# Three orders changed in a TensorE-bound chain of blocks: group norm at the scan's end, sums of a norm, fillers in windowed attention

## The reference, cut to what matters

```python
for i in range(DEPTH):                       # first block, DEPTH = 2
    if i < N_A_LAYERS:
        h = h + mamba2_mixer(h, ...)         # 4 groups: conv, chunked scan, gated group norm, out projection
    else:
        k_sh, v_sh = shared_kv(h, ...)
        h = h + swa_layer(h, k_sh, v_sh, ...)    # windowed attention, window 128, 16 heads
    h = h + per_layer_embedding(h, p[i], ...)    # sigmoid(rms_norm(h) @ gate_w) * (p_i @ proj_w)
# group norm of the mixer, per group of 512 channels
yg = yg * lax.rsqrt(jnp.mean(yg * yg, axis=-1, keepdims=True) + EPS)
# second block begins
h = rms_norm_2(x, ln1_g[i]); z = h @ w_in[i]
```

## Time and profile before

| | |
|---|---|
| median of 3 runs | 1419.25 us (1418.35 to 1421.17) |
| profiled execution | 1417.13 us |
| its span, first to last instruction | 1415.0 us |
| TensorE, matmuls busy | 1376.1 us, 97% |
| VectorE, ScalarE, GpSimd busy | 836.4, 661.4, 527.2 us |
| mean granted TensorE clock | 0.995 |

### The profile page before, as it was taken

The page is one execution under the profiler, slowest core; times in us unless marked ns, Lnnn a source line. Parts: engine busy times, 40 slices in busy tenths (PEclk is TensorE's granted clock), DMA queues, the critical chain, the costliest instruction groups (busy, mean ns, idle before and its releaser), DMA issues.

```text
span 1415.0 us, 18159 instructions
## 1 busy us (share of the span) xinstructions
PE 1376.1 (97%) x6776; PEld 1088.3 (77%) x6776; DVE 836.4 (59%) x1453; ACT 661.4 (47%) x1126; POOL 527.2 (37%) x259
## 2 busy tenths in 40 slices
PE   9999999999999999989999999999999999999998
PEld 6777878777778878856888887775677888888887
DVE  5576464757557764675576514367756654544755
ACT  6654634635455443585555412344555323232553
POOL 2553553635320034455100434124353555555200
PEclk9999999999999999999999999999999999999999
DMA  5322323222123223211334333130012323333331
GB/s 187 90 75 60 90 60 88 77 60 75 62 88 90 91 89 90 75 49 43 89 90 119 90 119 119 31 104 30 16 30 81 99 91 103 91 103 91 118 89 60
DMA packets 33078, 116.82 MB, mean 83 GB/s; under 512 B 3932, under 2 KB 4316, under 8 KB 32736
## 3 DMA queue, kind: packets, MB, share of 16 engines
q1 hardware_dynamic: 31976, 111.85, 26.2%
q10 hardware_dynamic: 1016, 3.81, 0.8%
HBM read 113.55 MB, written 2.10 MB: 82 GB/s over the span
## 4 chain that ended last, share of the span: by engine, by line
PE 88%; DVE 5%; ACT 3%; issue 2%; POOL 1%; DMA 1%; ACTq 0%; DVEq 0%
PE bank L1272 84%; PE bank L1730 1%; PE bank L1573 1%; ACT wsh L846 1%; DMA h<-in_xT 1%; POOL wsl L698 1%; DVE arena L1888 0%; PE bank L1445 0%; POOL arena L756 0%; PE bank L1480 0%; ACT arena L1208 0%; DVE arena L2260 0%; ACT arena L928 0%; DVE arena L1968 0%; POOL arena L779 0%
## 5 line engine op out<-in xcount | busy, mean ns | idle before, releaser
L698 POOL TENSOR_TENSOR wsl<-ring,wsh 128x1024 fp32r<-128x1024 f32 x144 | 349.6, 2429 | 569.0 <-ACT wsh L846 568.9
L846 ACT ACTIVATE wsh<-ring 128x1024 fp32r<-128x1024 f32 x199 | 210.6, 1058 | 493.3 <-PE bank L1272 470.8
L1272 PE MATMUL bank<-parts1h,wsh 128*128 128x512 f32 (+1 forms) x736 | 293.2, 398 | 8.2 <-DVE parts1l L1811 2.1
L1272 PE MATMUL bank<-parts0h,wsh 128*128 128x512 f32 x704 | 282.9, 402 | 3.7 <-issue 1.3
L1272 PE MATMUL bank<-parts1l,wsh 128*128 128x512 f32 (+1 forms) x736 | 286.3, 389 | 0.0
L1272 PE MATMUL bank<-parts1h,wsl 128*128 128x512 f32 (+1 forms) x736 | 286.2, 389 | 0.0
L1272 PE MATMUL bank<-parts0h,wsl 128*128 128x512 f32 x704 | 275.0, 391 | 0.0
L1272 PE MATMUL bank<-parts0l,wsh 128*128 128x512 f32 x704 | 274.7, 390 | 0.0
L1272 PEld LDWEIGHTS bank<-parts1h,wsh 128*128 128x128 f32 x736 | 138.9, 189 | 44.3 <-issue 4.3
L1272 PEld LDWEIGHTS bank<-parts0h,wsh 128*128 128x128 f32 x704 | 132.6, 188 | 38.4 <-issue 6.8
L1272 PEld LDWEIGHTS bank<-parts1h,wsl 128*128 128x128 f32 x736 | 138.9, 189 | 29.0
(11 more groups left out here) (313 smaller groups left out, 1823.1 us busy)
## 6 DMA issues: line engine op xcount, KB each, us to landing
ring<-in_wstream SPq DMA_DIRECT2D x206, 512.0 KB, 3.6
arena<-in_alibi ACTq DMA_DIRECT2D x2, 1024.0 KB, 5.1
outT<-arena SPq DMA_DIRECT2D x8, 256.0 KB, 2.6
h<-in_xT SPq DMA_DIRECT2D x2, 256.0 KB, 5.8
h<-in_xT ACTq DMA_DIRECT2D x2, 256.0 KB, 6.3
h<-in_xT SPq DMA_DIRECT2D x1, 512.0 KB, 8.5
h<-in_xT ACTq DMA_DIRECT2D x1, 512.0 KB, 9.3
arena<-in_cmpb ACTq DMA_DIRECT2D x1, 496.0 KB
```

The lines of the kernel that those rows point to most:

```text
L698: return nc.gpsimd.tensor_tensor(dst, src, hi.bitcast(F32), ALU.subtract)
L846: nc.scalar.activation(wsh[n % NSET][:, :], src, ACT.Copy).then_inc(*done("high", ("high", L)))
L1272: return nc.tensor.matmul(*args, **kw)
```

## The change

Three orders and one split of a step:

- Scan of group 3: `sout(2, 4)` moves into the scan's fillers. With nine fillers in place of eight they are spread anew, which puts `sout(2, 1)` ahead of `ssd2(3, 0)`, and `proj(3, 9)` and `psp(0)` each earlier by a step (`psp(0)` now ahead of `ssd2(3, 3)`). After the scan: `yt` x4, `sout(2, 5)`, `ya`, `sout(2, 6)`, `gn`, `sout(2, 7)`, `pp(0, 0)`, `gb`, `pp(0, 1)`, `pp(0, 2)`, `pp(0, 3)`. Before, it was `yt` x4, `sout(2, 4)` to `sout(2, 7)`, `gn`, `pp(0, 0)`, `pp(0, 1)`, `gb`, `pp(0, 2)`, `pp(0, 3)`.
- All groups: the last `yadd` leaves `gn` for a new step `ya`, one step after the beginning of `head`.
- Attention: `psp(1)` moves from behind the `aV` of unit 1 to ahead of the first `aT`; the four fillers `pp(1, m)` move from units 3, 4, 5, 6 to units 1, 2, 8, 9.
- `norm(4)` moves from behind `avg(0)` to behind `avg(1)`, `nb(4)` from behind `avg(1)` to behind `avg(2)`.

```diff
-            fill = nxt[7:8] + so[:2] + nxt[8:9] + so[2:4] + nxt[9:] + [("psp", 0)]
-            head, mid, tail = so[4:], [("pp", 0, 0), ("pp", 0, 1)], [("pp", 0, 2), ("pp", 0, 3)]
+            fill = nxt[7:8] + so[:2] + nxt[8:9] + so[2:4] + nxt[9:] + [("psp", 0)] + so[4:5]
+            head, mid, tail = so[5:7], so[7:] + [("pp", 0, 0)], [("pp", 0, m) for m in (1, 2, 3)]
...
-        out += [("yt", g, m) for m in range(GT)] + head + [("gn", g)] + mid + [("gb", g)] + tail
+        out += [("yt", g, m) for m in range(GT)] + head[:1] + [("ya", g)] + head[1:] + [("gn", g)] + mid + [("gb", g)] + tail
...
-    out += [("gate", 6)] + swa[:7] + [("gate", 7), ("qT", 1)]
-    between = {3 + m: [("pp", 1, m)] for m in range(4)} | {10 + m: [("ao", 0, m)] for m in range(6)}
+    out += [("gate", 6)] + swa[:7] + [("gate", 7), ("qT", 1), ("psp", 1)]
+    between = {u: [("pp", 1, m)] for m, u in enumerate((1, 2, 8, 9))} | {10 + m: [("ao", 0, m)] for m in range(6)}
...
-    out += body[:k] + [("psp", 1), ("half",)] + body[k:]
+    out += body[:k] + [("half",)] + body[k:]
...
-    out += [("avg", 0), ("norm", 4), ("avg", 1), ("nb", 4), ("avg", 2), ("avg", 3)] + [("cmp_in", 0), ("mif",), ("mrow",), ("cmp_in", 1)]
+    out += [("avg", 0), ("avg", 1), ("norm", 4), ("avg", 2), ("nb", 4), ("avg", 3)] + [("cmp_in", 0), ("mif",), ("mrow",), ("cmp_in", 1)]
...
-                if k == "gn":
+                if k == "ya":
                     yadd(a[0], 3)
```

## The result

The change makes the kernel faster: a median of 1411.41 us over 8 executions (1410.03 to 1415.96) against 1419.19 us over 8 of the kernel before (1416.42 to 1422.34), a ratio of 0.9943 with a 95% interval of 0.9931 to 0.9955. By the medians that is 7.8 us; 6.1 were predicted, 1413.1 us with a range of 1410.5 to 1417.0.

What follows compares the result with a forecast made beforehand. TensorE, busy 97% of the span, was taken as the bound, leaving its idle time and clock falls to gain. Scan 2.6, attention 1.3 and norm 4 2.2 sum to 6.1 us, giving a 1413.1 us median; range 1410.5 to 1417.0.

Steps and rivals of the forecast that it cites:

- `ssd2(3,0)`, 1.3 us: Scan of group 3: sout(2,1) ahead covers the 1.32 us wait for the masked decay; gain 1.3 us.
- `ssd3(3,3)`, a wait of 0.9 again: Scan of group 3: psp(0)'s subtraction now precedes the scaled term, so TensorE again waits 0.9 us; gain 0.
- `gn`, a wait of 1.5 against 1.47: End of group 3's scan: the last sum comes sooner but so does TensorE; wait 1.5 us against 1.47, gain 0.
- The clock falls at `gn` as before: After gn(3): the quiet stays as long (1.5 + 1.1 us), so the clock falls as before; gain 0, other end 1.7 us.
- `gb` to `sout(3,0)`, 1.3 us: Broadcast to sout(3,0): a third pp of 1.37 us fills the 1.3 us idle; gain 1.3 us.
- Attention, 1.3 us: Attention: 0.9 in the first units plus 1.5 at units 8 and 9, less 1.1 new idle in units 3 to 6.
- Norm 4, 2.2 us: Norm 4: 0.58 us idle before the sums goes and the clock holds, worth 1.6; gain 2.2 us, bounds 0.4 and 2.3.
- Rival 1: Clock holds at gn(3) as well: 1.7 us more gain, 1411.4 us; chance 0.17.
- Rival 2: Clock falls at norm 4 anyway, behind the two column sums: 1.7 us less gain, 1414.8 us; chance 0.15.
- Rival 3: Attention's unfilled units cost more than 1.1 us, latencies setting their pace: 3.5 us idle, 1415.6 us; chance 0.14.
- Rival 4: Attention's four unfilled units take 18.9 us without fillers too, losing 5.5 us: 2.4 us slower, 1421.7 us; chance 0.05.
- Rival 5: Moved steps only move the waits; just ssd2(3,0)'s 1.3 and the 0.6 between norm 4's sums stay: 1417.4 us; chance 0.07.

Runs made afterwards that it cites:

- Experiment 4: Kernel after with psp(0) moved one step later, behind ssd2(3,3): 1410.32 us, ratio 0.9934 against the kernel before.
- experiment 7: Kernel after without ya, the last sum of squares made at gn again: 1413.28 us, ratio 0.9951 against the kernel before.
- experiment 10: Kernel after with psp(1) one step later, behind the aT of unit 0: 1412.14 us, ratio 0.9946 against the kernel before.
- experiment 1: Kernel before with only the scan's new order and the step ya: 1414.53 us, ratio 0.9964 against the kernel before.
- Experiment 6: Kernel after with attention's four fillers back at units 3 to 6, psp(1) still early: 1414.04 us, ratio 0.9957 against the kernel before.
- experiment 8: Kernel after with attention's second filler at unit 5 in place of unit 2: 1410.84 us, ratio 0.9936 against the kernel before.
- experiment 2: Kernel before with only attention's new order: 1416.15 us, ratio 0.9981 against the kernel before.
- Experiment 5: Kernel after with gn(3) behind sout(2,7) again, ya staying where it is: 1411.72 us, ratio 0.9941 against the kernel before.
- experiment 9: Kernel after with psp(0) behind ssd2(3,3) and attention's fillers at units 1, 5, 8, 9: 1408.33 us, ratio 0.9924 against the kernel before.
- experiment 11: Kernel after with psp(0) behind ssd2(3,3), fillers at units 1, 5, 8, 9 and psp(1) behind unit 0's aT: 1408.43 us, ratio 0.9922 against the kernel before.
- experiment 3: Kernel before with only norm 4's new order: 1415.95 us, ratio 0.998 against the kernel before.

## Why the prediction was right, and where it was off

The direction and the places held, and the total came out. Of the three terms the scan's held in size (2.6 against 2.7), attention's was too small by 0.8 us, and norm 4's was too large by 0.65 in an execution without the fall. Those two errors cancel, so that the total is closer than its parts deserve, by luck. Step by step:

- **`ssd2(3,0)`, 1.3 us.** Right: no idle before it.
- **`ssd3(3,3)`, a wait of 0.9 again.** Right: 0.75, and for the reason given, the subtraction in front of the term. Experiment 4 shows it: with the subtraction behind the term the wait is 0. The chain to the last sum shortens with it, and the wait before `gn` falls from 1.25 to 0.70.
- **`gn`, a wait of 1.5 against 1.47.** Right in kind, 1.24 measured. That the two canceled was no accident: TensorE comes a block earlier and so does the sum, and experiment 7 shows the part that `ya` has in that (0.6 us).
- **The clock falls at `gn` as before.** True of this pair of profiles, but no property of the kernels. The old order fell in two of three profiled executions, the order of after in two of five (after and experiment 10; not in experiments 1, 6 and 8), and in the pair of after and experiment 1 it cost 1.6 us; in experiment 2, where it lasted twice as long, it cost 3.2. With the chance of 0.17 given to the other case the prediction was surer than one profile allows.
- **`gb` to `sout(3,0)`, 1.3 us.** Right: no stall behind the third `pp`. Experiment 5 shows that what stands between `gn` and `gb` matters as well: with `pp(0,0)` alone there, and a split ahead of the root, the broadcast waits 1.86 us.
- **Attention, 1.3 us: the term that was mis-sized.** It measured 2.09.
  - The opening gave waits of 1.61 + 0.23 = 1.84 where 1.7 + 0.7 = 2.4 were worked out: the step "It waits 0.7" before `aT(1,0)` was too much by 0.5. From the start of the first `aV` to that `aT` the product was to take 5.0 us and took 4.7 (601.88 to 606.60), and TensorE's own work was to take 4.3 and took 4.5: a `pp` between `aS` and `aV` takes 1.58 us from its first matmul to that of the `aV` (604.12 to 605.71 and 608.68 to 610.26 in after), and the prediction had 1.37, from a block of such matmuls.
  - Units 8 and 9 gave back all of their 2.0 us and not 1.5. The units without fillers lost 1.79 us and not 1.1; VectorE's busy time of 14.47 us was only a bound from below for their pace: the waits in after end with ScalarE's copy (L1100) and GpSimd's product (L756), the last links of a chain over all the engines.
  - By the listed waits the net is 5.48 - 3.86 = 1.6 us. Most of the other 0.5 lies in the distances between TensorE's starts: at a listed wait the distance grows by some 0.07 us (once 0.14) more than the idle that is listed, of which before has one wait more, and before has three delays of 0.1 to 0.2 us that are too short for the list (at 605.84, 609.92 and 632.62) where after has one. Counted by starts, before loses 6.4 us there and after 4.4.
  - Experiment 6 shows which half made the gain: the fillers (1.6 to 2.0), hardly the earlier `psp(1)` (0.45 at most).
- **Norm 4, 2.2 us.** 2.16 in the profiled pair. But the prediction's 0.58 of idle and 1.6 of clock hold only for an execution with the fall. Without it the old order has 0.58 before the sums and 0.70 before the broadcast, and the part is worth 1.55. The diagonal's margin in the new order was worked out as 0.8 us; the diagonal is there at 757.79 (757.10 and 0.69) and TensorE comes at 758.67, 0.9 later. Two splits and the two small transfers stood ahead of the root on ScalarE, and it held all the same.
- **The sum.** 6.1 predicted; 6.9 by the three segments of the profiled pair, 6.4 with no falls, 6.7 at equal clocks.

The prediction weighed a rule of the Trainium skill (TensorE: Matmul & The Clock Gate, Part 1: The HAM clock gate), that the activity window runs freely and does not restart with the kernel. The runs agree with it: the order of before fell at norm 4 in one profiled execution and, in experiments 1 and 2, which have the same order there, did not. They show that the same order falls in some executions and not in others; that a free-running window is the reason they do not show. By that rule the sum was to be 4.4 us, with the whole fall taken off. Without falls it came to 6.4: attention gave 0.8 more than its term, and at norm 4 the old order pays 0.70 us at the broadcast when the clock holds, so that a fall there costs it 0.6 us and not 1.7.

Rival 1 came about in three of five profiles of the new order. Rival 2 did not in any of ten. Rival 3 was right in kind: the unfilled units cost more than 1.1 us, and what their waits end with is not VectorE; its size, 3.5 us, was too much. Rivals 4 and 5 did not come about. Rival 4 needed 4.8 us lost in the four units, and those show 1.8 us of idle in all. (The window of 18.10 us was chosen to span them with work around them; it isn't the same work as the 18.9 us of the earlier trace rows.)

The median of after is 1.7 us below the prediction. The sum free of falls accounts for 0.3 of it. The other 1.4 lie inside the interval of the ratio, which is 6.4 to 9.8 us, and the runs don't say more about them. The step from the profiled execution to the median was a guess that did not hold: the prediction took the median to lie 2.1 us above the profiled execution for both kernels, and for after it lies 1.2 below.

## What to carry to other kernels

Where TensorE is busy throughout, an order is judged by two questions at each wait: which instruction stands ahead, in its own engine's queue, of the one that ends the wait, and what that one itself waits for. One loss left in the scan of after was a subtraction that waited for a ScalarE copy directly ahead of a term that TensorE needed; moving it behind the term gave 1.4 us. The wait of 1.61 us before the first `aV` is still there. Fillers belong where the chain through the other engines is longest against TensorE's own work, and where two helpers are busy for 75 and 77% of a stretch, its fillers will be missed when they are taken away, here by 1.8 us of idle against the 5.5 at which the prediction priced them.

## What the runs showed of the hardware

**Falls of the clock vary between executions of the same order.** In the thirteen profiled executions (before, after and the eleven experiments), at five places where TensorE is quiet:

| place | profiles with a fall |
|---|---|
| `gn(3)`, old order | 2 of 3 |
| `gn(3)`, order of after (idle 1.24 us, then 1.0 us of column sums) | 2 of 5 |
| `gn(3)`, experiment 7 (idle 1.87 us) | 1 of 1 |
| `gn(3)`, experiments 4, 9 and 11 (idle 0.7 us) | 0 of 3 |
| `gn(3)`, experiment 5 (no idle before the sums) | 0 of 1 |
| norm 4, old order | 1 of 3 |
| norm 4, new order | 0 of 10 |
| first units of attention, old order | 0 of 3 |
| the same, `psp(1)` ahead of the first `aT` | 3 of 8 |
| the same, `psp(1)` behind the first `aT` (experiments 10 and 11) | 0 of 2 |
| some 11 us, unchanged (after, experiments 3, 10 and 11) | 4 of 13 |
| 84 to 87 us, unchanged, idle 2.5 us | 3 of 13 |

The change takes one fall away at norm 4 and may bring one in attention, where the old order showed none. Three profiles of the old order there are too few to tell. If it comes in 3 of 8 executions and 1.3 us of it come through, as in experiments 2 and 7 (both have an attention segment of 103.05 us), it costs the change some 0.5 us on average; that is an estimate from those two figures.

The last row is the fall that the prediction missed with its "the clock stayed at 1.00 over 84 to 87 us": it comes there too, in experiments 5, 6 and 8. Windows of experiment 8 at that place:

```profile
82.00:86.00 4.00, 1.70 (x8) 1.08 (x6) 3.29 (x12) 2.21 (x3) 1.07 (x1) 1.00 0.26 107
86.00:90.00 4.00, 3.82 (x16) 3.16 (x17) 3.93 (x6) 2.71 (x5) 2.85 (x2) 0.65 0.32 105
```

**A fall can come and last with TensorE busy.** In the profile of after it ran without a gap from 912 us on, with two groups of column sums at 918 to 920.7, and the clock fell at 922 and stayed at 1.2 GHz until some 932.6. Windows of after:

```profile
916.00:918.00 2.00, 2.00 (x10) 1.48 (x9) 1.93 (x6) 0.92 (x3) 0.44 (x1) 1.00 0.84 227
918.00:920.00 2.00, 2.00 (x14) 1.50 (x13) 1.03 (x3) 0.15 (x1) 1.71 (x3) 1.00 0.73 162
...
922.00:924.00 2.00, 2.00 (x17) 1.94 (x16) 0.00 (x0) 2.00 (x4) 0.00 (x0) 0.60 0.81 172
```

This one fall lost 5.1 us, three times the usual. With the next one it is 8.5 us, 5.1 more than the two falls of before in that stretch, and it cost the span 2.2 more, because the waits that follow shrank: the wait for ScalarE (L1219) at 959 to 964 us is 1.40 us in before and 0.51 in after, and one of 0.93 us for VectorE (L2431) behind it is gone. Why the falls are longer there in after the runs do not show. The order in that stretch is the same in all thirteen profiles: experiments 2, 3, 4, 8 and 11 had only two falls of 1.7 in it, as before had, experiment 9 the same 5.1 and 3.4 as after, and experiment 10 three, of 5.1, 1.7 and 3.4.

**The same subtraction, two durations.** The 128x1024 subtraction of `psp(1)` on VectorE took 2.48 us before, from 608.81, beside a product of GpSimd (608.31, 1.89 us). Moved to where GpSimd is idle it took 1.22:

```profile
601.29 1.22 DVE L1787 TENSOR_TENSOR parts0l<-ring,parts0h 128x1024 fp32r<-128x1024 f32 x1 [2.21 <-ACT parts0h L841]
```

The prediction had priced it at 1.23. No experiment moved the neighbour alone, but the trace of before has 58 subtractions of this line and size. The 55 with no GpSimd instruction beside them took 1.21 to 1.23 us each, and the three with one beside them 1.46, 2.48 and 2.59. All three end 1.1 us after the GpSimd instruction does, as if they had begun only then. The longest of them, beside a GpSimd subtraction (L698) that runs from 1321.47 for 2.40 us, is this:

```profile
1322.37 2.59 DVE L1787 TENSOR_TENSOR parts1l<-ring,parts1h 128x1024 fp32r<-128x1024 f32 x1 [1.41 <-ACT parts1h L841]
```
